# Three 64-byte gaps that move the split weights and the shared SBUF region of a one-core decoder kernel

## The chip, the cores and the metric

The kernel runs on one core of one Trainium2 chip. The metric is the device time in microseconds; the time before is the median of three runs, and one more execution was profiled.

## The reference

A trunk of two decoder layers on x of 256 rows by 1024 columns, float32. Each layer has a mixing part (RMSNorm, one input projection, a convolution group, an attention group, an output projection) and a channel part: a dense SwiGLU in layer 0, and in layer 1 a SwiGLU of which each row uses 2 of 8 experts.

```python
def swiglu(h, w1, w3, w2):
    return (jax.nn.silu(h @ w1) * (h @ w3)) @ w2

for layer in range(2):
    h = rms_norm(x, attn_norm_g[layer])
    z = h @ w_in[layer]
    ...
    x = x + jnp.concatenate([conv_out, attn_out], axis=-1) @ w_out[layer]
    h = rms_norm(x, ffn_norm_g[layer])
    if layer % 2 == 0:
        x = x + swiglu(h, dense_w1[i], dense_w3[i], dense_w2[i])    # 1024 -> 2816 -> 1024
    else:
        x = x + moe_swiglu(h, router_w[i], moe_w1[i], moe_w3[i], moe_w2[i])   # 8 experts, 1024 -> 3584 -> 1024
```

## The kernel before

All weights stream from HBM through `ring`, four slots of 16 KB a partition, which in the dense and the expert stage serve as seven pieces of 128 x 2048 float32. The SP queue issues the DMAs in one fixed order, each as soon as the piece's last tenant is used up.

The mixing parts use plain F32 matmuls on the ring, hT, mixT and the arena (L1120, L1163, L1309). The dense and the expert stage use F32R matmuls, in which each operand is split in a high and a low part and three products stand for one: high x high, high x low, low x high. For each piece ACT casts the high part into `w_hi` (L484), DVE subtracts it from the piece into `w_lo` (L734), and PE uses both. There are three buffers of each (`SPLIT` = 3): ACT waits for `w_used` of three pieces ago, DVE for ACT, PE for DVE. The order of this work on ACT and DVE is written out by hand, with the other work of the stage put between.

The operands that PE takes, written as stationary / moving:

- dense up, 352 of each line L1329 to L1331: a 128-column slice of w_hi or w_lo / hT_hi or hT_lo, 256 columns
- dense down, 88 of each line L1345 to L1347: a slice of dact_hi or dact_lo / w_hi or w_lo, 512 columns
- expert up, 896 of each line L1428 to L1430: a slice of xe_hi or xe_lo / w_hi or w_lo, 512 columns
- expert down, 448 of each line L1450 to L1452: a slice of actT_hi or actT_lo / w_hi or w_lo, 512 columns
- gather, L1384: a slice of h_hi or h_lo / sel, 256 columns
- scatter, L1403 and L1404: a slice of selT / ye_hi or ye_lo, 512 columns

Twelve matmuls use up one piece in expert up and down. Between the chunks stand transposes (L1438, L1101, which also fill waits so that PE stays busy).

SBUF tiles are laid out one behind the other in the order in which `sb` names them, each at the next multiple of 32 bytes in its partition: ring, w_hi, w_lo, x_sb, hn, hT, then the parameters, constants and small tables, the last of them vc. Behind vc comes one region that three sets of tiles share in turn: mixT and the arena for the mixing parts, hT_hi, hT_lo, dact_hi and so on for the dense stage, and h_hi, h_lo, xe_hi, xe_lo, actT_hi, actT_lo, ye_hi, ye_lo, sel, selT for the expert stage. All tiles there but the last have a size that is a multiple of 128 bytes, except the arena, which ends its set.

Of the kernel before, what the change touches and what calls it, by code (L numbers as in the profile page):

```python
# [5 lines left out]
P = 128  # L6
# [11 lines left out]
def hymba_trunk(nc, x, w_in, cmp_k_w1, cmp_v_w1, w_out, dense_w1, dense_w3, dense_w2,  # L18
# [74 lines left out]
    with ctx:  # L93
        def sb(name, shape, dt=F32):
            return ctx.enter_context(nc.sbuf_tensor(name, shape, dt))
# [2 lines left out]
            return ctx.enter_context(nc.semaphore(name))  # L98

        ring = sb("ring", [P, SLOTS * SLOT])  # L100
        w_hi = [sb(f"w_hi{n}", [P, PIECE], F32R) for n in range(SPLIT)]
        w_lo = [sb(f"w_lo{n}", [P, PIECE], F32R) for n in range(SPLIT)]
        x_sb = sb("x_sb", [P, NT, D])
        hn = sb("hn", [P, NT, D])
        hT = sb("hT", [P, KD, S])
# [36 lines left out]
        vc = sb("vc", [P, HD])  # L142


        attention_phase, dense_phase, expert_phase = ExitStack(), ExitStack(), ExitStack()


# [1404 lines left out]
```

How the kernel before makes its waits and increments, by code:

```python
        def wait_slot(eng, kind, l, c):  # L296
            n = slot_of[kind, l, c]
            eng.wait_ge(slot_arrived[n % SLOTS], 16 * turn_of[kind, l, c])
# [8 lines left out]
        def wait_raw(eng, t, j=None):  # L308
            eng.wait_ge(piece_arrived[t % RAW], nth(j, 16 * XS // RAW, 16 * (t // RAW + 1)))
# [24 lines left out]
        @block.sync  # L335
# [2 lines left out]
                sp.dma_start(x_sb[:, i, :], x[i * P:(i + 1) * P, :]).then_inc(x_loaded, 16)  # L338
            tenant = {}
            for key in stream:
                if key in slot_of:
                    n = slot_of[key]
                    parts, dst, arrived = (2 * (n % SLOTS), 2 * (n % SLOTS) + 1), slot(n), slot_arrived[n % SLOTS]
                else:
                    t = piece_of[key]
                    parts, dst, arrived = (t % RAW,), raw(t), piece_arrived[t % RAW]
                for before_it in dict.fromkeys(tenant[q] for q in parts if q in tenant):
                    sp.wait_ge(*last_read(before_it))
                tenant.update({q: key for q in parts})
                src, k, m = source(*key)
                dst = dst[:, 0:k * m].rearrange("p (k n) -> p k n", k=k)
# [9 lines left out]
            def stream_expert(j, e, first):  # L361
# [6 lines left out]
                    if first and m < RAW:  # L368
                        for before_it in dict.fromkeys([tenant[t % RAW]]):
                            sp.wait_ge(*last_read(before_it))
                    else:
                        sp.wait_ge(w_lo_ready, j * XS + (t - RAW + 1))
                    if kind == "e2":
```

## Time and profile before

| | us |
|---|---|
| median of 3 runs | 1643.5 (1641.4 to 1645.4) |
| the profiled execution | 1643.6 |
| its span | 1641.6 |
| PE busy | 1586.6 |
| DVE busy | 1194.1 |
| ACT busy | 908.1 |

The span runs from the first to the last instruction. PE is TensorE's matmuls, PEld its weight loads, DVE is VectorE, ACT ScalarE, POOL GpSimd. The two mixing parts lie at 0 to 200 and 400 to 600 us, the dense stage at 205 to 400, the expert stage at 615 to 1640. Matmuls overlap, and the end of each is modelled; what one costs is read from the distance between the starts of two that follow each other without a wait.

### The profile page before, as it was taken

To read this page: it belongs to the slowest core of one execution; us is meant where nothing else is said; L and a number is where in the kernel's file an instruction comes from. 1 tells how busy PE (TensorE), PEld (TensorE's weight loads), DVE (VectorE), ACT (ScalarE), POOL (GpSimd) and SP (SyncE) were. 2 spreads that over 40 slices of the span, in tenths; PEclk is the share of its full clock that TensorE was granted. 3 is DMA by queue.
4 is the path that set the end of the run, shared out by engine and by line. 5 is a ranking of instruction groups with operands and counts; after the bars stand their busy time and mean duration, and the time that the engine had idled before them with its cause. 6 is when DMAs were issued, how large, how long until landed. Compare 5 with 4: busy or idle time off the path is not lost.

```text
span 1641.6 us, 19740 instructions
## 1 busy us (share of the span) xinstructions
PE 1586.6 (97%) x7328; PEld 1227.3 (75%) x7328; DVE 1194.1 (73%) x1156; ACT 908.1 (55%) x834; POOL 24.0 (1%) x42
## 2 busy tenths in 40 slices
PE   7998999998999899999999999999999999999998
PEld 5663499997755367888887888887888887888886
DVE  4965155444775437889888889887889887888885
ACT  1034243342004316777777777777777777677674
POOL 1010000000010000000000000000000000000000
PEclk9978999999997799999999999999999999999999
DMA  7510195526070037999998999998999998999992
GB/s 242 197 37 0 44 340 180 182 100 196 15 254 27 0 129 253 361 366 346 357 371 304 359 366 351 357 367 301 364 363 347 363 360 318 356 360 358 356 347 99
DMA packets 203555, 426.56 MB, mean 260 GB/s; under 512 B 7378, under 2 KB 48594, under 8 KB 203476
## 3 DMA queue, kind: packets, MB, share of 16 engines
q1 hardware_dynamic: 202160, 424.90, 72.8%
q8 instruction: 64, 1.05, 0.3%
q10 hardware_dynamic: 1316, 0.49, 0.1%
q14 instruction: 15, 0.12, 0.0%
HBM read 424.31 MB, written 1.05 MB: 259 GB/s over the span
## 4 chain that ended last, share of the span: by engine, by line
PE 91%; DVE 4%; issue 2%; ACT 2%; DMA 1%; POOL 0%; ACTq 0%; POOLq 0%; DVEq 0%; SPq 0%
PE bank L1428 13%; PE bank L1430 13%; PE bank L1429 13%; PE bank L1120 8%; PE bank L1450 6%; PE bank L1452 6%; PE bank L1451 6%; PE bank L1309 3%; PE bank L1329 3%; PE bank L1331 3%; PE bank L1330 2%; PE bank L1264 2%; PE bank L1438 1%; PE bank L1345 1%; PE bank L1347 1%
## 5 line engine op out<-in xcount | busy, mean ns | idle before, releaser
L734 DVE TENSOR_TENSOR w_lo<-ring,w_hi 128x2048 fp32r<-128x2048 f32 x369 | 843.6, 2291 | 225.3 <-ACT w_hi L484 225.1
L484 ACT CAST w_hi<-ring 128x2048 fp32r<-128x2048 f32 x369 | 704.9, 1913 | 319.8 <-PE bank L1430 181.7
L1428 PE MATMUL bank<-w_hi,xe_hi 128*128 128x512 f32 x896 | 360.6, 402 | 6.8 <-DVE w_lo L734 6.8
L1429 PE MATMUL bank<-w_lo,xe_hi 128*128 128x512 f32 x896 | 355.0, 396 | 0.0
L1430 PE MATMUL bank<-w_hi,xe_lo 128*128 128x512 f32 x896 | 354.9, 396 | 0.0
L1428 PEld LDWEIGHTS bank<-w_hi,xe_hi 128*128 128x128 f32 x896 | 169.0, 189 | 46.6 <-DVE w_lo L734 8.4
L1430 PEld LDWEIGHTS bank<-w_hi,xe_lo 128*128 128x128 f32 x896 | 169.0, 189 | 41.2
L1429 PEld LDWEIGHTS bank<-w_lo,xe_hi 128*128 128x128 f32 x896 | 169.2, 189 | 38.1
L1450 PE MATMUL bank<-w_hi,actT_hi 128*128 128x512 f32 x448 | 177.8, 397 | 0.0
L1451 PE MATMUL bank<-w_lo,actT_hi 128*128 128x512 f32 x448 | 177.0, 395 | 0.0
L1452 PE MATMUL bank<-w_hi,actT_lo 128*128 128x512 f32 x448 | 177.0, 395 | 0.0
L1452 PEld LDWEIGHTS bank<-w_hi,actT_lo 128*128 128x128 f32 x448 | 84.1, 188 | 20.5
L1450 PEld LDWEIGHTS bank<-w_hi,actT_hi 128*128 128x128 f32 x448 | 84.2, 188 | 19.7
L1451 PEld LDWEIGHTS bank<-w_lo,actT_hi 128*128 128x128 f32 x448 | 84.2, 188 | 19.7
L1329 PE MATMUL bank<-hT_hi,w_hi 128*128 128x256 f32 x352 | 98.4, 280 | 0.0
L1330 PE MATMUL bank<-hT_lo,w_hi 128*128 128x256 f32 x352 | 98.1, 279 | 0.0
L1331 PE MATMUL bank<-hT_hi,w_lo 128*128 128x256 f32 x352 | 98.1, 279 | 0.0
L757 DVE SCALAR_TENSOR_TENSOR arena<-arena,par 128x256 f32<-128x256 f32 x240 | 96.2, 480 | 0.1
L729 DVE TENSOR_TENSOR x_sb<-x_sb,bank 128x512 f32<-128x512 f32 x48 | 30.3, 683 | 66.8 <-PE bank L1309 60.0
L1120 PE MATMUL bank<-ring,hT 128*128 128x512 f32 (+1 forms) x192 | 72.3, 531 | 0.0
L1329 PEld LDWEIGHTS bank<-hT_hi,w_hi 128*128 128x128 f32 x352 | 66.1, 188 | 0.4
L1330 PEld LDWEIGHTS bank<-hT_lo,w_hi 128*128 128x128 f32 x352 | 65.9, 187 | 0.4
(228 smaller groups left out, 1457.7 us busy)
## 6 DMA issues: line engine op xcount, KB each, us to landing
ring<-in_moe_w SPq DMA_DIRECT2D x336, 1024.0 KB, 5.7
ring<-in_dense_w SPq DMA_DIRECT2D x33, 1024.0 KB, 5.4
ring<-in_w_in SPq DMA_DIRECT2D x8, 1024.0 KB, 9.6
ring<-in_w_in SPq DMA_DIRECT2D x4, 2048.0 KB, 14.3
ring<-in_w_out SPq DMA_DIRECT2D x4, 2048.0 KB, 14.3
ring<-in_cmp_k_w SPq DMA_DIRECT2D x2, 2048.0 KB, 17.2
ring<-in_cmp_v_w SPq DMA_DIRECT2D x2, 2048.0 KB, 8.8
ring<-in_w_in SPq DMA_DIRECT2D x2, 1120.0 KB, 15.6
```

The lines of the kernel that those rows point to most:

```text
L484: nc.scalar.copy(w_hi[t % SPLIT][:], raw(t)).then_inc(w_hi_ready, 1)
L734: V.tensor_tensor(w_lo[t % SPLIT][:], raw(t), w_hi[t % SPLIT][:].bitcast(F32), ALU.subtract).then_inc(w_lo_ready, 1)
L1120: last = T.matmul(dst, lhs(k), rhs(k), start=(n == 0), stop=(n == len(chunks) - 1))
L1329: T.matmul(dst, hi[:, k, c], hT_hi[:, k, :], start=(k == 0), stop=False)
L1330: T.matmul(dst, hi[:, k, c], hT_lo[:, k, :], start=False, stop=False)
L1331: last = T.matmul(dst, lo[:, k, c], hT_hi[:, k, :], start=False, stop=(k == KD - 1))
L1428: T.matmul(dst, xe_hi[:, kk, own], hi[:, k, :], start=(kk == 0), stop=False)
L1429: T.matmul(dst, xe_hi[:, kk, own], lo[:, k, :], start=False, stop=False)
L1430: last = T.matmul(dst, xe_lo[:, kk, own], hi[:, k, :], start=False, stop=(kk == KD - 1))
L1450: T.matmul(dst, actT_hi[:, c % 2, f], hi[:, k, r], start=first, stop=False)
L1451: T.matmul(dst, actT_hi[:, c % 2, f], lo[:, k, r], start=False, stop=False)
L1452: last = T.matmul(dst, actT_lo[:, c % 2, f], hi[:, k, r], start=False, stop=end)
```

## The change

Three tiles of 64 bytes a partition that nothing reads or writes are allocated: one between the ring and the split weights, one between the split weights and x_sb, and one between vc and the region that the stages share. With them the split weights begin 64 bytes above a multiple of 128, where they began at one, and the shared region begins at a multiple of 128. x_sb and all up to vc move by 128 bytes.

```diff
         ring = sb("ring", [P, SLOTS * SLOT])
+        sb("split_gap", [P, 16])
         w_hi = [sb(f"w_hi{n}", [P, PIECE], F32R) for n in range(SPLIT)]
         w_lo = [sb(f"w_lo{n}", [P, PIECE], F32R) for n in range(SPLIT)]
+        sb("x_gap", [P, 16])
         x_sb = sb("x_sb", [P, NT, D])
...
         vc = sb("vc", [P, HD])


+        sb("gap", [P, 16])
         attention_phase, dense_phase, expert_phase = ExitStack(), ExitStack(), ExitStack()
```

## Rows read from the trace of the kernel before

**Rows 1.** The page: busy us of each engine, share of the span, instructions
```profile
PE 1586.6 (97%) x7328; PEld 1227.3 (75%) x7328; DVE 1194.1 (73%) x1156; ACT 908.1 (55%) x834; POOL 24.0 (1%) x42
```
**Rows 2.** Stretches; columns: stretch, us, busy by engine, PEclk, DMA share, GB/s
```profile
185.00:330.00 145.00, 143.62 (x1008) 129.03 (x1007) 69.94 (x52) 57.76 (x47) 1.11 (x2) 1.00 0.66 216
...
640.00:1640.00 1000.00, 990.02 (x4446) 801.21 (x4444) 851.16 (x510) 714.73 (x510) 0.00 (x0) 1.00 0.95 342
```
**Rows 3.** Groups by line and shape: count, busy us, mean ns, idle before
```profile
L734 DVE TENSOR_TENSOR w_lo<-ring,w_hi 128x2048 fp32r<-128x2048 f32 x369 | 843.6, 2291 | 225.3 <-ACT w_hi L484 225.1
...
L1428 PE MATMUL bank<-w_hi,xe_hi 128*128 128x512 f32 x896 | 360.6, 402 | 6.8 <-DVE w_lo L734 6.8
...
L1450 PE MATMUL bank<-w_hi,actT_hi 128*128 128x512 f32 x448 | 177.8, 397 | 0.0
...
L1329 PE MATMUL bank<-hT_hi,w_hi 128*128 128x256 f32 x352 | 98.4, 280 | 0.0
...
L1345 PE MATMUL bank<-w_hi,dact_hi 128*128 128x512 f32 x88 | 34.8, 395 | 0.0
```
**Rows 4.** Timeline of PE and PEld, expert up: start us, us, instruction; five matmuls left out
```profile
700.01 0.39 PE L1429 MATMUL bank<-w_lo,xe_hi 128*128 128x512 f32 x1
700.01 0.19 PEld L1430 LDWEIGHTS bank<-w_hi,xe_lo 128*128 128x128 f32 x1
...
701.41 0.39 PE L1429 MATMUL bank<-w_lo,xe_hi 128*128 128x512 f32 x1
```
**Rows 5.** Timeline of PE, dense down; two matmuls left out
```profile
269.73 0.39 PE L1345 MATMUL bank<-w_hi,dact_hi 128*128 128x512 f32 x1
...
270.43 0.39 PE L1345 MATMUL bank<-w_hi,dact_hi 128*128 128x512 f32 x1
```
**Rows 6.** Timeline of PE, dense up, first stretch; five matmuls left out
```profile
212.01 0.28 PE L1329 MATMUL bank<-hT_hi,w_hi 128*128 128x256 f32 x1
...
212.69 0.28 PE L1329 MATMUL bank<-hT_hi,w_hi 128*128 128x256 f32 x1
```
**Rows 7.** Timeline of PE, dense up, a later stretch; eight matmuls left out
```profile
259.88 0.28 PE L1329 MATMUL bank<-hT_hi,w_hi 128*128 128x256 f32 x1
...
260.94 0.28 PE L1329 MATMUL bank<-hT_hi,w_hi 128*128 128x256 f32 x1
```
**Rows 8.** Timeline of PE, scatter and what follows; four matmuls left out
```profile
761.30 0.39 PE L1404 MATMUL bank<-ye_lo,selT 128*128 128x512 f32 x1
...
762.43 0.40 PE L1428 MATMUL bank<-w_hi,xe_hi 128*128 128x512 f32 x1
```
**Rows 9.** Timeline of PE, gather, merged by the view
```profile
613.80 1.00 PE L1384 MATMUL bank<-sel,h_hi 128*128 128x256 f32 x7
614.64 1.12 PE L1384 MATMUL bank<-sel,h_lo 128*128 128x256 f32 x8
```
**Rows 10.** Timeline of PE, plain F32 matmuls of the input projection
```profile
51.92 7.07 PE L1120 MATMUL bank<-hT,ring 128*128 128x256 f32 x32
```
**Rows 11.** Single lines of DVE and ACT: ns min/median/max, first and last start
```profile
L757 DVE SCALAR_TENSOR_TENSOR arena<-arena,par x240: 468/480/486, 32.1 to 496.5; 128x256 f32<-128x256 f32 x120
...
L935 DVE TENSOR_TENSOR hT_lo<-hT,hT_hi x4: 686/690/691, 204.3 to 206.1; 128x512 fp32r<-128x512 f32 x4
...
L942 DVE TENSOR_TENSOR dact_lo<-dact,dact_hi x11: 684/685/695, 223.9 to 385.5; 128x512 fp32r<-128x512 f32 x11
...
L591 ACT CAST hT_hi<-hT x4: 617/619/622, 202.6 to 204.4; 128x512 fp32r<-128x512 f32 x4
...
L600 ACT CAST dact_hi<-dact x11: 612/614/622, 221.8 to 384.9; 128x512 fp32r<-128x512 f32 x11
```
**Rows 12.** Timeline of DVE and PE, expert down: a piece ready and used
```profile
901.66 2.29 DVE L734 TENSOR_TENSOR w_lo<-ring,w_hi 128x2048 fp32r<-128x2048 f32 x1 [0.35 <-ACT w_hi L484]
...
905.11 0.39 PE L1450 MATMUL bank<-w_hi,actT_hi 128*128 128x512 f32 x1
```
**Rows 13.** One stretch of 2 us, the DMA's GB/s last
```profile
900.00:902.00 2.00, 2.00 (x10) 1.64 (x9) 1.65 (x3) 1.63 (x1) 0.00 (x0) 1.00 1.02 413
```

## The prediction

> **What bounds the kernel now.** I first read the page's busy times: PE is busy for 1586.6 us, 97% of the span [rows 1]. The table by stretches then separates the stages. In the expert stage PE is busy for 990 of 1000 us at clock 1.00 (the 2.4 GHz level), DVE for 851, ACT for 715. In the dense stage, 185 to 330 us, PE is busy for 143.6 of 145 [rows 2]. So each nanosecond of the spacing of PE's matmuls there is a nanosecond of the span, unless a feeder becomes late. The groups say how many there are [rows 3]: L1428 to L1430 have 896 each and L1450 to L1452 448 each, 4032 matmuls of 512 columns in the expert stage; L1345 to L1347 have 88 each, 264 of 512 columns in the dense stage; L1329 to L1331 have 352 each, 1056 of 256 columns. The idle time before L1428, the largest PE group, is 6.8 us in all.
>
> The mean of one matmul in those groups (402 ns) is not its cost, since matmuls overlap. The cost is the distance between starts, from the timeline.
>
> **What the change moves.** It has no instruction, wait or DMA more or less. By the change's own words the six split-weight tiles go from 0 to 64 bytes above a multiple of 128, and the shared region goes to 0. The tiles between them (x_sb to vc) take 41,792 bytes, each rounded up to 32; that is 326.5 times 128, so before it the shared region lies at 64. The ring, x_sb, hn and hT lie at 0 before and after (x_gap puts the last three back). Every slice that a matmul takes starts a multiple of 512 bytes into its tile, so a tile's place is that of all its slices.
>
> The split matmuls (F32R) have these places before, written as stationary/moving operand:
> - expert up and down, and dense down: 64/0 (xe, actT or dact / weights), 512 columns. In the timeline 6 matmuls take 1.40 us from start to start, 0.2333 each [rows 4], and 0.70 for 3, 0.2333 [rows 5].
> - dense up: 0/64 (weights / hT_hi, hT_lo), 256 columns. In the first stretch, entered from the 50 transposes, 0.68 for 6, 0.1133 [rows 6]; in the later ones, entered from dense down, 1.06 for 9, 0.1178 [rows 7]. One instruction stream with two spacings at one clock and with the same tiles: two things inside PE meet in step, and which step depends on how the stretch was entered. What PE reads together are the moving operand and the next stationary one: the LDWEIGHTS of L1430 starts with the matmul of L1429 [rows 4].
> - scatter: 64/64 (selT / ye), 512 columns: settles at 1.13 for 5, 0.226 [rows 8].
> - gather: 64/64 (h / sel), 256 columns: 0.84 for 7, 0.120 [rows 9].
>
> After it, expert up, expert down and dense down are 0/64, dense up is 64/0, scatter and gather are 0/0.
>
> **The cost of a matmul, split.** Scatter and gather have the same places and differ by 256 columns: 0.226 - 0.120 = 0.106 us for 256 columns, and that is 256 clocks of 2.4 GHz (0.1067), one for each column; the 0.014 left is then the same at both widths. Expert up and dense up differ by 0.2333 - 0.1178 = 0.1155, more than the clocks: either their pairs differ in the extra, or it grows with columns. Taking 0.106 or 0.212 off the others leaves, per matmul: 64/0 0.0213; 0/64 0.0073 or 0.0118; 64/64 0.014. So the placement with the moving operand at 0 costs most, and the one with it at 64 and the stationary one at 0 costs least. I take the first of the two readings, an extra for each weight load beside a running stream that depends on the pair, because at 64/64 it doesn't grow.
>
> **The sum**, against the profiled execution (span 1641.6 us, run 1643.6, median of the runs 1643.5, so the run stands for the median):
> - 4032 + 264 = 4296 matmuls of 512 columns go from 64/0 to 0/64. This pair with 512 columns is not in the trace. Bounds: 0.212 + 0.0073 = 0.2193 below and 0.240 above (twice gather's 0.120). I take 0.212 + 0.0118 = 0.2238, from the nearest row that is entered like most of them, out of other split matmuls. Gain 0.0095 x 4296 = 40.8 us (60.1 at 0.2193).
> - 1056 matmuls of dense up go from 0/64 to 64/0, also not in the trace with 256 columns. Now they cost 192 x 0.1133 + 864 x 0.1178 = 123.5 us. With the extra of 64/0, 0.106 + 0.0213 = 0.1273, they cost 134.4: a loss of 10.9. Half of 0.2333, 0.1167, is the other bound: 123.2, a gain of 0.3. I take the loss, since it follows from the same reading as the gain.
> - 160 gather and 72 scatter matmuls go to 0/0. Between 0.0073 and 0.0213 of extra against 0.014 now, that is 1.6 us either way; I take 0.
> - The plain F32 matmuls of the attention stages: 256 columns take 7.07 us for 32, about 0.22 each, twice the F32R price [rows 10]. Columns pass at half the rate there, and L1120 has hT and the ring both at 0, unmoved. Those on mixT and the arena move by 64 bytes against the ring; I take 0.
> - DVE and ACT: the 240 taps of L757 start at every fourth byte and take 468 to 486 ns. A subtraction with inputs at 0 and 64 has a median of 690 ns, with both at 64 685; a cast from 0 to 64 619, from 64 to 64 614 [rows 11]. So L734 and L484, which now go from the ring at 0 to weights at 64, change by some 5 ns (of 2291 for L734 [rows 3]). That hides under PE: one w_lo piece is written by 903.95 and PE comes to it at 905.11, 1.16 us later [rows 12]. Two pieces of 12 matmuls pass between the release of a buffer and its need; with 0.2238 that shortens the time by 24 x 0.0095 = 0.23 us and leaves 0.9.
> - DMA writes the ring where it did. A piece of 1.05 MB per 12 matmuls is 374 GB/s now and 390 at 0.2238; one 2 us stretch reached 413 [rows 13]. The mean over the stage would go from 342 to some 356. This doesn't bind; at 0.2193 (398 in such stretches) it comes near.
>
> Net: 40.8 - 10.9 = 29.9, so 1643.6 - 29.9 = 1613.7 us. With 0.2193 it is 1643.6 - 60.1 + 10.9 = 1594.4. If the place of the stationary operand doesn't matter (extra 0.014, spacing 0.226), the gain is 0.0073 x 4296 - 10.9 = 20.5: 1623.1. The forecast's own range is 1594 to 1625.
>
> **The rivals.**
> Same. Only whether the two operands lie on the same or on different halves counts, and 64/0 and 0/64 are different halves alike. Then the extra at different halves grows with columns (0.0213 at 512, 0.0073 to 0.0118 at 256, about half), and the change swaps one for the other: 1643 to 1644 us. For it: dense up is close to half of expert up (0.1178 x 2 = 0.2356, 0.1133 x 2 = 0.2267, around 0.2333). Against it: a cost that grows with columns for one pair and not for the other is an odd law.
> The Trainium skill would also have it so. "SBUF — State Buffer", Who interferes with whom, says that PE never waits on anyone at its two independent read ports, and "TensorE: Matmul & The Clock Gate", Back-to-back issue gap, gives N/2.4 + 2.5 ns, 215.8 ns for 512 columns warm, whatever the addresses. The trace doesn't agree: 233.3 ns at granted clock 1.00 [rows 2, 4], and 226 in another placement [rows 8]. By the pages' rule the change does nothing.
>
> Slower. The extra goes with the pair 0/64 in proportion to the columns, at the rate of dense up's later stretches: 2 x 0.1178 = 0.2356 for 512. The place is the 4296 long matmuls: 0.0023 x 4296 = 9.9 us, less 0.3 in dense up: 1653.2. At gather's rate, 0.240, it is 0.0067 x 4296 = 28.8: 1672. It decides as soon as the long matmuls settle above 0.2333. For it: dense up's later stretches are nine of ten.
>
> Faster by another law. Proportional too, but in the step of dense up's first stretch: 2 x 0.1133 = 0.2266, a gain of 0.0067 x 4296 = 28.8, 1615, without a loss in dense up.
>
> **How the numbers follow.** Forecast 0.43, faster by the other law 0.10, same 0.29, slower 0.18. A measurement of this kernel can tell about 0.2% (3.3 us) from no change: faster by more than that 0.53, within it 0.29, slower 0.18. The likeliest case gives 1614. The range goes from 1592, a little under the forecast's low end, to 1652, nearly the nearer point of the slower case: beyond it lies most of the slower case, 0.14, and below it 0.03.
>
> **What would show it.** Starts of L1428 to L1430 at 0.219 to 0.226 apart (same: 0.2333; slower: 0.2356 and up); L1345 to L1347 alike; L1329 to L1331 at 0.127 (by the other laws 0.117); DVE's and ACT's durations as before; PE's idle time before L1428 still under some 10 us. If that idle time grows with DVE or DMA named, the feeders took the gain. What would make the forecast wrong is the step from 256 columns to 512: that the extra of 0/64 is paid once per weight load is read off the 64/64 rows and carried over.

## The result, and the profile after

| | before | after |
|---|---|---|
| median, us | 1642.45 (4 runs, 1641.33 to 1645.38) | 1621.79 (4 runs, 1613.29 to 1625.08) |
| the profiled execution, us | 1643.6 | 1624.96 |
| its span, us | 1641.6 | 1622.9 |

The ratio is 0.9872, with a 95% interval of 0.9833 to 0.9911: the change makes the kernel 20.7 us faster at the medians. A second measurement (e6) gives 1621.13 against 1640.83, ratio 0.9883 (0.9854 to 0.9913).

The three new lines push the code down, so L1428 of before is L1431 here, L1450 is L1453, L1329 is L1332, L1345 is L1348, L734 is L737. The page's busy times, which answer to [rows 1]:

```profile
PE 1567.8 (97%) x7328; PEld 1225.5 (76%) x7328; DVE 1193.3 (74%) x1156; ACT 906.1 (56%) x834; POOL 24.0 (1%) x42
```

PE lost 18.8 us of busy time, and the span 18.7. DVE, ACT and the number of instructions are as before. The stretch of the expert stage that answers to the second line of [rows 2], and the groups that answer to [rows 3]:

```profile
640.00:1640.00 1000.00, 971.30 (x4435) 799.24 (x4433) 848.10 (x506) 712.47 (x510) 0.00 (x0) 1.00 0.94 341
```
```profile
L737 DVE TENSOR_TENSOR w_lo<-ring,w_hi 128x2048 fp32r<-128x2048 f32 x369 | 843.0, 2290 | 207.5 <-ACT w_hi L487 207.3
L487 ACT CAST w_hi<-ring 128x2048 fp32r<-128x2048 f32 x369 | 702.5, 1906 | 303.6 <-PE bank L1433 172.6 <-PE bank L1455 75.4 <-PE bank L1334 27.9
L1431 PE MATMUL bank<-w_hi,xe_hi 128*128 128x512 f32 x896 | 357.3, 399 | 7.0 <-DVE w_lo L737 7.0
```

The granted clock is 1.00 as before. The stretch now reaches past the end of the kernel, so PE's 971.3 us are no idle time. DVE's subtraction takes 2290 ns (2291 before), and PE's idle time before the largest group is 7.0 us (6.8): no feeder became late. What changed is the spacing of starts. The timeline of PE, expert down and then dense up (start us, duration us; 14 and 11 matmuls left out):

```profile
699.70 0.40 PE L1453 MATMUL bank<-w_hi,actT_hi 128*128 128x512 f32 x1
...
703.13 0.39 PE L1453 MATMUL bank<-w_hi,actT_hi 128*128 128x512 f32 x1
```
```profile
262.75 0.28 PE L1332 MATMUL bank<-hT_hi,w_hi 128*128 128x256 f32 x1
...
264.11 0.28 PE L1332 MATMUL bank<-hT_hi,w_hi 128*128 128x256 f32 x1
```

15 long matmuls take 3.43 us, 0.2287 each, where [rows 4, 5] have 0.2333. 12 of dense up take 1.36, 0.1133 each, where [rows 7] have 0.1178. Over all matmuls, starts behind a wait or a transpose left out, the means from start to start are 229.2 ns in expert up, 229.0 in expert down, 228.9 in dense down (233.3 in all three before), and 113.6 in dense up (117.1 before). So the long ones give (233.3 - 229.1) x 4296 = 18 us and dense up (117.1 - 113.6) x 1056 = 3.7 us, 21.7 in all. From the first to the last expert matmul the time falls from 1007.6 to 991.5 us (16.1), from the first to the last of dense up from 173.9 to 169.4 (4.5, with the dense down in it). The rest of the difference of the two spans, 1.9 us the other way, lies in the mixing parts, whose time differs by more than that from one execution of a kernel to the next: from the last matmul of the dense stage to the first gather it is 218.8 us in this execution of the changed kernel and 213.8 in e6's.

Gather has kept its 0.120: in the timeline around 611 us twelve start in 1.44 us.

### The profile page after: what moved, and what is told of

It reads as the page before. It is cut to its first block, busy times and chain, and to the rows that moved or that the text cites. A ratio compares the mean times of both kernels' runs of the same rounds, so it can differ in the third digit from the quotient of the medians.

```text
span 1622.9 us, 19740 instructions
## 1 busy us (share of the span) xinstructions
PE 1567.8 (97%) x7328; PEld 1225.5 (76%) x7328; DVE 1193.3 (74%) x1156; ACT 906.1 (56%) x834; POOL 24.0 (1%) x42
## 4 chain that ended last, share of the span: by engine, by line
PE 90%; DVE 4%; ACT 2%; issue 2%; DMA 1%; POOL 0%; ACTq 0%; POOLq 0%; DVEq 0%; SPq 0%
PE bank L1431 13%; PE bank L1433 13%; PE bank L1432 13%; PE bank L1123 8%; PE bank L1455 6%; PE bank L1453 6%; PE bank L1454 6%; PE bank L1312 3%; PE bank L1332 2%; PE bank L1334 2%; PE bank L1333 2%; PE bank L1267 2%; PE bank L1441 2%; PE bank L1235 1%; PE bank L1350 1%
## 5 line engine op out<-in xcount | busy, mean ns | idle before, releaser
L737 DVE TENSOR_TENSOR w_lo<-ring,w_hi 128x2048 fp32r<-128x2048 f32 x369 | 843.0, 2290 | 207.5 <-ACT w_hi L487 207.3
L487 ACT CAST w_hi<-ring 128x2048 fp32r<-128x2048 f32 x369 | 702.5, 1906 | 303.6 <-PE bank L1433 172.6
L1431 PE MATMUL bank<-w_hi,xe_hi 128*128 128x512 f32 x896 | 357.3, 399 | 7.0 <-DVE w_lo L737 7.0
L1432 PE MATMUL bank<-w_lo,xe_hi 128*128 128x512 f32 x896 | 351.2, 392 | 0.0
L1431 PEld LDWEIGHTS bank<-w_hi,xe_hi 128*128 128x128 f32 x896 | 169.1, 189 | 42.8 <-DVE w_lo L737 8.5
L1453 PE MATMUL bank<-w_hi,actT_hi 128*128 128x512 f32 x448 | 176.1, 393 | 0.0
L1332 PE MATMUL bank<-hT_hi,w_hi 128*128 128x256 f32 x352 | 97.4, 277 | 0.0
L1453 PEld LDWEIGHTS bank<-w_hi,actT_hi 128*128 128x128 f32 x448 | 84.2, 188 | 17.3
L1332 PEld LDWEIGHTS bank<-hT_hi,w_hi 128*128 128x128 f32 x352 | 66.1, 188 | 0.4
```

Source lines behind the costliest of these rows:

```text
L487: nc.scalar.copy(w_hi[t % SPLIT][:], raw(t)).then_inc(w_hi_ready, 1)
L737: V.tensor_tensor(w_lo[t % SPLIT][:], raw(t), w_hi[t % SPLIT][:].bitcast(F32), ALU.subtract).then_inc(w_lo_ready, 1)
L1332: T.matmul(dst, hi[:, k, c], hT_hi[:, k, :], start=(k == 0), stop=False)
L1431: T.matmul(dst, xe_hi[:, kk, own], hi[:, k, :], start=(kk == 0), stop=False)
L1432: T.matmul(dst, xe_hi[:, kk, own], lo[:, k, :], start=False, stop=False)
L1453: T.matmul(dst, actT_hi[:, c % 2, f], hi[:, k, r], start=first, stop=False)
```

## Experiments

Below, a place is a byte address modulo 256. The distance of a matmul is the place of its stationary operand less that of its moving one, modulo 256. This is not how the prediction looked at it, but it is what the runs led to:

| kernel | weights | region | long matmuls, distance | dense up, distance |
|---|---|---|---|---|
| before | 128 | 192 | 64 | 192 |
| after | 192 | 128 | 192 | 64 |
| e1: weights alone | 192 | 64 | 128 | 128 |
| e2: region alone | 128 | 0 | 128 | 128 |
| e3: all by 128 | 0 | 64 | 64 | 192 |

The expectations of e1, e2, e5, e7 and e8 take the places of e1 or e2 for distance 0. That was my error: modulo 128 both tiles lie at one place, modulo 256 they lie 128 apart.

**Parts of the change.** e1 leaves out the gap ahead of the region, e2 keeps only that one, e3 has one gap of 128 bytes ahead of the weights and keeps every place modulo 128.

```diff
 # e1, against the kernel after
-        sb("gap", [P, 16])
 # e2, against the kernel after
-        sb("split_gap", [P, 16])
-        sb("x_gap", [P, 16])
 # e3, against the kernel before
+        sb("split_gap", [P, 32])
```

> The third gap is left out: the split weights go to 64, the shared region stays at 64, so all split matmuls are 64/64 (stationary/moving). Pair theory (each pair of places has its own spacing): the long matmuls come near the scatter row of before, 0.226 to 0.2296, span 1612 to 1627; dense up near gather, 0.120, 3 us more than before. Moving-operand theory (only the place of the moving operand counts, 64 is the good one for 512 columns): the long ones 0.229 as with both changes, span 1623 or less. Relative theory (only same or different halves, or the distance between the two): another spacing than the 0.229 of the full change, since here the distance is 0.

> Only the third gap: the weights stay at 0, the shared region goes to 0, so all split matmuls are 0/0. Pair theory: a spacing of its own, between 0.219 and 0.240. Moving-operand theory: the long matmuls stay at 0.2333, span 1640 to 1644. Relative theory: the same spacing as with the weights alone moved (distance 0 in both), for the long and for the dense-up matmuls.

> One gap of 128 bytes ahead of the split weights: all but the ring moves by 128, so the halves stay 64/0 and 0/64 as before, and only the place modulo 256 turns. If the place modulo 128 is what counts: 0.2333 and 0.1133 to 0.1178, time as before within 0.2%. If the place modulo 256 or the distance to the ring counts: another spacing, or other durations on DVE and ACT.

e1: 1638.16 us, ratio 1.0008 (0.9975 to 1.0042). e2: 1636.55, ratio 0.9987 (0.9969 to 1.0005). e3: 1640.71, ratio 0.9998 (0.9977 to 1.0018); before 1641.4. Neither half of the change makes a measurable difference alone. The long matmuls (those of 512 columns) have means of 232.2 to 233.1 ns in e1, 232.2 to 232.5 in e2, 233.3 in e3; dense up is at 118.7, 118.7 and 117.1. Weights and region each moved on their own bring no gain, the two together do: what counts is a relation between the two operands, not the place of either. e3 has the spacings of before to 0.1 ns, so moving weights and region together by 128 is free.

**The price of pairs.** e4 puts nineteen trains of 96 equal matmuls behind the last scatter of the kernel before, where ACT, DVE and the DMA queues are idle. A train is one uninterrupted row of matmuls, entered from four transposes (`keep_busy`); its settled spacing is the mean from start to start once it repeats itself. The first train:

```diff
+            keep_busy(4, 4)
+            for _ in range(96):
+                T.matmul(bank[0][0:128, 0:512], probe_s[:, 0:128], probe_w[:, 0:512], start=True, stop=True)
...
```

> The kernel before, with 19 trains of 96 equal F32R matmuls appended on PE behind the last scatter, each entered from four transposes: eleven pairs of places of stationary and moving operand at 512 columns, four at 256, and two with a stationary operand of 32 columns instead of 128; nothing else runs then. About 390 us longer. Pair theory with an extra per weight load: 64/0 at 512 columns 0.2333, 0/64 0.224 to 0.229, 64/64 0.226; at 256 columns the same extras (0.127, 0.113, 0.120); with 32-column loads the extra falls to a quarter. Extra that grows with columns: 0.1167 at 256 columns, and 0.2333 with 32-column loads too. Relative theory: trains of the same distance but other places have the same spacing. If DVE, ACT or DMA make the extra, all trains come at 0.2133 to 0.216.

Four trains, by line (columns: duration ns min/median/max, first and last start us):

```profile
L1501 PE MATMUL bank<-w_hi,xe_hi x96: 393/396/478, 1630.2 to 1652.4; 128*128 128x512 f32 x96
...
L1507 PE MATMUL bank<-w_hi,xe_hi x96: 388/392/481, 1675.8 to 1697.7; 128*128 128x512 f32 x96
...
L1510 PE MATMUL bank<-w_hi,xe_hi x96: 387/389/476, 1698.2 to 1719.9; 128*128 128x512 f32 x96
...
L1552 PEld LDWEIGHTS bank<-w_hi,xe_hi x96: 107/108/112, 1971.3 to 1993.2; 128*32 128x32 f32 x96
L1552 PE MATMUL bank<-w_hi,xe_hi x96: 391/396/478, 1971.3 to 1993.4; 128*32 128x512 f32 x96
```

Stationary and moving operand lie at 448 and 128 (modulo 512) in L1501, at 64 and 128 in L1507, at 128 and 128 in L1510. The settled spacings are 233.3, 228.9 and 226.7 ns. L1501 and L1507 are one pair of halves, 64 and 0 modulo 128, and differ by 4.4 ns: the reading by halves is wrong. All trains of 512 columns at 32-byte places agree with the distance: 64 gives 233.3 (448/128, 448/384 has 64 too, 0/192), 192 gives 228.9 (64/128, 128/192, 128/448), 0 gives 226.7 (128/128, 448/448, 448/192), 128 gives 233.4 (0/128). L1552 loads 32 columns of weights in place of 128. The load takes 108 ns, not 188, yet the train settles at 231.7: the extra does not shrink with the load, and is no fixed price for each one. The other train with 32-column loads has distance 192 and settles at 231.7 too, so with the short load these two distances, 4.4 ns apart with the full one, make no difference.

**The distances.** e5 has the form of the kernel: three products to a slice, both operands walking in steps of 512 words, at twelve distances and three widths. The first train:

```diff
+            for n in range(32):
+                k, m = 512 * (n % 3) + 48, 512 * (n % 3)
+                for sv, wv in ((ph, wh), (ph, wl), (pl, wh)):
+                    T.matmul(bank[0][:, 0:512], sv[:, k:k + 128], wv[:, m:m + 512], start=True, stop=True)
...
```

> The kernel before with 23 trains of 96 matmuls behind the last scatter, each in the expert's own pattern (high x high, high x low, low x high, on changing slices of xe and w): twelve distances stationary minus moving modulo 256 at 512 columns, eight at 256, three at 384. Distance theory (formed after the single-pair trains: distance 0 226.7, 64 233.3, 128 233.4, 192 228.9 ns at 512 columns; 64 113.3, 192 117.8, 0 120.0 at 256): distances 64, 128 and 192 repeat these numbers in the pattern, and the distances between give values of their own. If the 232.5 ns of the region-only kernel at distance 0 come from the pattern of three products, distance 0 gives about 232.5 here too; if they come from DVE, ACT or DMA working beside PE, it gives 226.7. Extra per column: 384 columns at distance 64 175.0, at 192 171.7. Extra per matmul: 180.0 at 64 and 175.5 at 192.

Timeline of PE, distances 0, 64 and 192 at 512 columns (11 matmuls left out of each pair):

```profile
1647.40 0.39 PE L1503 MATMUL bank<-w_lo,xe_hi 128*128 128x512 f32 x1
...
1650.12 0.39 PE L1503 MATMUL bank<-w_lo,xe_hi 128*128 128x512 f32 x1
...
1714.52 0.40 PE L1518 MATMUL bank<-w_hi,xe_lo 128*128 128x512 f32 x1
...
1717.32 0.40 PE L1518 MATMUL bank<-w_hi,xe_lo 128*128 128x512 f32 x1
...
1827.36 0.39 PE L1543 MATMUL bank<-w_lo,xe_hi 128*128 128x512 f32 x1
...
1830.11 0.39 PE L1543 MATMUL bank<-w_lo,xe_hi 128*128 128x512 f32 x1
```

Twelve matmuls take 2.72, 2.80 and 2.75 us: 226.7, 233.3 and 229. The whole table of settled spacings, in ns:

| distance | 0 | 16 | 32 | 64 | 96 | 128 | 160 | 176 | 192 | 208 | 224 | 240 |
|---|---|---|---|---|---|---|---|---|---|---|---|---|
| 512 columns | 226.7 | 226.7 | 233.3 | 233.3 | 234.3 | 233.4 | 233.3 | 230.1 | 228.8 | 233.3 | 233.3 | 226.7 |
| 384 columns | 173.3 | | | 174.7 | | | | | 173.3 | | | |
| 256 columns | 120.0 | | 118.4 | 113.3 | 118.7 | 118.7 | 120.1 | | 117.8 | | 116.7 | |

Taking the clocks of the columns off (N/2.4 at granted clock 1.00), distance 0 leaves 13.3 ns at all three widths. Distance 64 leaves 6.6, 14.7 and 20.0 at 256, 384 and 512 columns, distance 192 leaves 11.1, 13.3 and 15.5. So the extra is neither one price nor in proportion: it depends on distance and width together. The best distance for 256 columns (64) is among the worst for 512. One train stands behind each cell. The values of 0, 64 and 192 at 512 columns came again in each train of e4, e7 and e11 that has these distances at places that are multiples of 32 bytes; for 16, 128 and 240 the runs below show a second value each.

**Is it the company?** In the kernel DVE, ACT and the queues write SBUF beside PE. e7 runs trains alone and beside DVE subtractions, ACT casts and 1 MB DMAs into the ring, one by one and together. ACT's part beside the third train:

```diff
...
+            sc.wait_ge(go, 3)
+            for q in range(10):
+                nc.scalar.copy(w_hi[2][:], raw(1)).then_inc(abusy, 1)
+                sc.wait_ge(abusy, 0 + q + 1)
...
```

> The kernel before with 14 trains of 96 matmuls of 512 columns in the expert's pattern behind its end, at one distance each, alone or beside nine DVE subtractions (D), ten ACT casts (A), eight DMAs of 1 MB into the ring (S) of the kernel's own kind. Theory that the 232.5 ns of the region-only kernel at distance 0 are the doing of another engine beside PE: distance 0 gives 226.7 alone and about 232.5 beside the one that disturbs it, and 64 and 192 stay at 233.3 and 228.9 with all three. Rival: the other engines do nothing (the rule that PE waits on nobody), and distance 0 gives 226.7 in all five trains; then the kernel's 232.5 is a step that PE fell into by how it was entered.

Two stretches of trains at distance 192, first beside all three, then beside the DMAs alone or none (busy us of PE, PEld, DVE, ACT, POOL; granted clock, DMA share, GB/s), and the timeline of PE in the first:

```profile
1888.00:1906.00 18.00, 18.00 (x81) 14.75 (x80) 17.76 (x8) 17.71 (x10) 0.00 (x0) 1.00 0.78 272
1866.00:1884.00 18.00, 18.00 (x81) 14.75 (x80) 0.00 (x0) 0.00 (x0) 0.00 (x0) 1.00 0.66 233
```
```profile
1895.42 0.39 PE L1699 MATMUL bank<-w_lo,xe_hi 128*128 128x512 f32 x1
...
1898.16 0.39 PE L1699 MATMUL bank<-w_lo,xe_hi 128*128 128x512 f32 x1
```

The second stretch was meant to be alone, but its trace has DMA traffic of 233 GB/s, left over from the train before; e4 and e5 have the same spacings with no traffic at all. PE starts 81 matmuls in 18 us in both, with DVE and ACT busy throughout in one and idle in the other. With nothing else at work (e5) and beside all three: 226.7 and 226.7 at distance 0, 233.3 and 233.3 at 64, 228.8 and 228.9 at 192; distance 0 keeps 226.7 beside each of the three alone as well. At these distances the spacing is PE's own affair. For two others that isn't shown. Distance 128 settles at 232.4 beside all three where e5 has 233.4, and distance 240 at 228.3 where e5 has 226.7, on the same addresses. Neither ran alone in e7. Both hold their value from the first microsecond to the last, and other runs below have two values at one distance with nothing beside PE, so a second rhythm is as likely a reason as the company. Here the Trainium skill holds ("SBUF — State Buffer", Who interferes with whom: PE waits on nobody), as far as other engines go at those three distances. That the two read ports which the same section gives PE are independent is what the trains don't bear out: with PE alone at work, another relation of its two operands' addresses costs 7 ns more.

**Gains that the distance promises.** e9 is the changed kernel with two more gaps, so that the long matmuls have distance 0 and dense up keeps its 64. e10 puts weights and region at one place, 192, so that all have 0. e8 has distance 16, which was as good as 0 in e5, with the weights at 176 and all behind them 256 bytes further on.

```diff
 # e9, against the kernel after
         hT_hi, hT_lo = ...
+        sb_d("dense_gap", [P, 16])
         dact_hi, dact_lo = ...
         h_hi, h_lo = ...
+        sb_e("expert_gap", [P, 16])
         xe_hi = ...
 # e10, against the kernel after
-        sb("x_gap", [P, 16])
+        sb("x_gap", [P, 48])
-        sb("gap", [P, 16])
 # e8, against the kernel before: tiles that may start at 16 bytes
+        sb("split_gap", [P, 12])
-        w_hi = [sb(f"w_hi{n}", [P, PIECE], F32R) for n in range(SPLIT)]
...
+        w_hi = [sb16(f"w_hi{n}") for n in range(SPLIT)]
...
```

> The split weights 48 bytes above their place of before and everything behind them 256 bytes, so that the long matmuls have distance 16 modulo 256, and dense up 240. If a train's spacing alone carries over: 226.7 for the long matmuls, 28 us less than before, dense up some 3 us more, span about 1615. If distances near 0 are disturbed in the kernel as 0 was: 232 to 233, span 1635 to 1642.

> The changed kernel with two more gaps of 64 bytes, one ahead of dact_hi and one ahead of xe_hi: the long matmuls get distance 0 modulo 256 (all places multiples of 32 bytes), dense up keeps 64. Distance theory: long 226.7, dense up 113.3; 4296 x 2.2 ns less than the changed kernel is 9.5 us, so about 1612, ratio to before 0.981 to 0.984. If the long ones don't settle at 226.7 in the kernel (as at distance 16, where they came at 233.3 and 236.7), 1620 to 1650.

> Weights 64 bytes on, everything behind them 256 bytes on: distance 0 modulo 256 in all split matmuls, both operands at the same place. Distance theory: long 226.7, dense up 120.0: 28.4 less, 2.8 to 3.1 more, about 1617. Half theory (same half 64/64): what the weights-only kernel gave, 1634 to 1640.

e9: 1618.98 us, ratio 0.9866 (0.9849 to 0.9883). e10: 1617.25, ratio 0.9861 (0.9828 to 0.9894). e8: 1647.52, ratio 1.0036 (1.0021 to 1.0051). First and last start of expert up in before, after, e9 and e10 (L1428 under the line number of each):

```profile
L1428 PE MATMUL bank<-w_hi,xe_hi x896: 393/394/797, 623.4 to 1615.1; 128*128 128x512 f32 x180
```
```profile
L1431 PE MATMUL bank<-w_hi,xe_hi x896: 388/394/795, 621.0 to 1596.7; 128*128 128x512 f32 x180
```
```profile
L1433 PE MATMUL bank<-w_hi,xe_hi x896: 388/390/792, 624.3 to 1593.2; 128*128 128x512 f32 x180
```
```profile
L1430 PE MATMUL bank<-w_hi,xe_hi x896: 387/389/795, 622.2 to 1589.7; 128*128 128x512 f32 x180
```

991.7, 975.7, 968.9 and 967.5 us: the expert stage is 7 to 8 us shorter than in the changed kernel, as 226.7 against 228.9 ns promises, and the means there are 227.0 to 227.6. But e10 pays 120.0 ns in dense up, 6.4 x 1056 = 7 us back, and e9 did not keep its 113.3. Dense up in e9, first stretch and a later one (8 and 11 matmuls left out):

```profile
214.15 0.28 PE L1336 MATMUL bank<-hT_hi,w_lo 128*128 128x256 f32 x1
...
215.17 0.28 PE L1336 MATMUL bank<-hT_hi,w_lo 128*128 128x256 f32 x1
```
```profile
262.83 0.28 PE L1336 MATMUL bank<-hT_hi,w_lo 128*128 128x256 f32 x1
...
264.24 0.28 PE L1336 MATMUL bank<-hT_hi,w_lo 128*128 128x256 f32 x1
```

0.1133 in the first, 0.1175 in the later one, with w_hi and hT_hi at the very places of the changed kernel. All nine later stretches settle at 117.8, which costs 9 x 96 x 4.4 = 3.8 us. e10 came out as its spacings promise. e9 came out 7 us above the 1612 that was expected of it: these 3.8, and some 3 us because its long matmuls have means of 226.9 to 227.6 and not 226.7. Neither kernel is shown to beat the changed one: the three ratios' intervals overlap.

e8 is slower than before where its distance promised a gain, and shows that a train doesn't always speak for the kernel. Between one group of transposes and the next lie 164 stretches of expert matmuls, 12 to 48 long; 99 of them settle at 236.7 ns and 65 at 233.3:

```profile
699.76 0.40 PE L1457 MATMUL bank<-w_hi,actT_lo 128*128 128x512 f32 x1
...
703.31 0.40 PE L1457 MATMUL bank<-w_hi,actT_lo 128*128 128x512 f32 x1
```

15 matmuls in 3.55 us. e11 asked whether 16-byte places are a case of their own.

```diff
...
+                k, m = 512 * (n % 3) + 0, 512 * (n % 3) + 12
...
```

> Ten trains of 96 matmuls of 512 columns in the expert's pattern behind the kernel before, at places (stationary, moving) modulo 256. Theory from the distance-16 kernel: distance alone counts only while the moving operand starts at a multiple of 32 bytes. (192,192) 226.7, (208,192) 226.7, (192,176) 233.3 to 236.7, (176,176) and (144,128) tell whether the moving or the stationary operand has to be so placed; (192,132) above 236, (196,128) near 233; (64,128) 228.9, (64,144) above it. If only the distance counts: (192,176), (208,192) and (144,128) all 226.7.

Partly. Stationary/moving at 192/176, the places of e8, gives 226.7 again, so the train still doesn't show what the kernel does. But distance 16 at 208/192 and at 144/128 gives 233.4, and distance 0 at 176/176 gives 230.0 against 226.7 at 192/192. At 192/132, the moving operand 4 bytes past a multiple of 16, it is 240.0; at 196/128, the stationary one 4 bytes past, 231.4. But the train at 144/128 is e5's train of distance 16 over again: the same instructions on the same addresses, entered from four transposes, with nothing beside PE. There it settled at 226.7. First e5, then e11, 11 matmuls left out of each pair:

```profile
1668.25 0.39 PE L1508 MATMUL bank<-w_lo,xe_hi 128*128 128x512 f32 x1
...
1670.97 0.39 PE L1508 MATMUL bank<-w_lo,xe_hi 128*128 128x512 f32 x1
...
1712.00 0.40 PE L1518 MATMUL bank<-w_lo,xe_hi 128*128 128x512 f32 x1
...
1714.80 0.40 PE L1518 MATMUL bank<-w_lo,xe_hi 128*128 128x512 f32 x1
```

2.72 against 2.80 us for twelve. So neither the distance nor the places settle the spacing here, and e8's miss need not be a matter of 16-byte places: a train shows one rhythm of those that its addresses allow. Ahead of the four transposes stood a train at 226.7 in e5 and one at 230.0 in e11.

**Two rhythms at one distance.** e12 asks what e9's dense up has that the changed kernel's has not. Its trains have dense up's form at distances 64 and 192 and start behind transposes alone or behind eighteen long matmuls of four distances.

```diff
...
+            keep_busy(4, 4)
+            long(0, 16)    # eighteen of 512 columns, distance 0
+            for n in range(32):
+                k = 256 * (n % 7)
+                for wv, hv in ((wh, ph), (wh, pl), (wl, ph)):
+                    T.matmul(bank[0][:, 0:256], wv[:, k + 32:k + 32 + 128], hv[:, k:k + 256], start=True, stop=True)
...
```

> The kernel before with thirteen trains of 96 matmuls of 256 columns behind its last scatter, in the dense up's form (stationary a slice of the split weights, moving the split activations, three products to a slice). The question is why the dense up of the two-distances kernel settled at 117.8 ns and that of the changed kernel at 113.4, with w_hi and hT_hi at the same places (distance 64) in both, and why in the kernel before the first stretch has 113.3 and the nine others 117.8 at one distance (192). The trains at distance 64 and at distance 192 start behind four transposes alone, or behind eighteen matmuls of 512 columns at distance 0, 64, 192 or 128. If the distance alone sets the spacing: 113.3 in all trains at 64, 117.8 in all at 192, whatever stands ahead. If one distance carries two rhythms and the matmuls ahead choose between them: at 64, 117.8 behind distance 0 and 113.3 behind distance 192; at 192, 117.8 behind distance 64; some of the others differ among themselves. If something else in the kernel does it (the buffers of the down matmuls, the waits): one value a distance, as under the first. In two trains (64 behind 0, 192 behind 64) a matmul of 384 columns stands in the middle: under two rhythms the spacing may change there, under distance alone it is the same on both sides. At distance 0 behind distance 64: 120.0 under both.

Distance 64, behind long matmuls of distance 0 (L1514) and of distance 64 (L1520), 11 left out of each pair:

```profile
1657.20 0.28 PE L1514 MATMUL bank<-xe_hi,w_lo 128*128 128x256 f32 x1
...
1658.62 0.28 PE L1514 MATMUL bank<-xe_hi,w_lo 128*128 128x256 f32 x1
...
1673.09 0.28 PE L1520 MATMUL bank<-xe_hi,w_hi 128*128 128x256 f32 x1
...
1674.45 0.28 PE L1520 MATMUL bank<-xe_hi,w_hi 128*128 128x256 f32 x1
```

1.42 against 1.36 us for twelve, the same instructions on the same addresses. At distance 64 the train settles at 113.3 behind transposes, behind 64 and behind 128, at 117.8 behind 0 and behind 192, and keeps it to its end; a matmul of 384 columns put in the middle doesn't move it. At distance 192 all trains have 117.8. So one distance can carry two stable rhythms, and what stood ahead chooses between them. This is e9's case: its dense down has distance 0. It is no full law. In the changed kernel dense up at 64 comes behind dense down at 192 and has 113.4 where the train has 117.8, and in the kernel before the first stretch at 192 has 113.3 [rows 6], a rhythm that no train at 192 took. Nor is it only the short ones: in the changed kernel 3 of the 164 expert stretches settle at 233.3 and the others at 228.6 to 229.2, and the train at 144/128 has both 226.7 and 233.3.

**The changed kernel again**, in a second measurement:

> The changed kernel again, on one chip with many runs of the kernel before: ratio 0.983 to 0.991 if the first measurement holds. If the gain hangs on the chip or on how PE falls into step in one execution, it differs from that.

1621.13 us, ratio as given at the top; 229.2, 229.0, 228.8 and 113.6 ns, as in the first measurement.

## Why the prediction was right, and where it was not

1614 was forecast with a range of 1592 to 1652; 1621.8 came out, faster, inside the forecast's own range. The steps:

- **PE sets the end, and each nanosecond of spacing counts**: right. 18.8 us of PE's busy time went, 18.7 of the span, and the idle time before the largest group is 7.0, 6.8 before.
- **DVE, ACT, DMA, gather at nothing**: right. 2290 against 2291 ns for the subtraction, 1906 against 1913 for the cast, 347 against 348 GB/s between 640 and 1620 us, gather 0.120.
- **The cost of a matmul, split.** This is the step that failed. It took the extra as a price for each weight load that depends on the pair of halves modulo 128. e4 has two trains with one pair of halves and 4.4 ns between them (L1501 and L1507), and a weight load of 108 ns in place of 188 that leaves the extra nearly whole. What the runs show in its place, for places at multiples of 32 bytes, is the distance of the two starts modulo 256, with a different extra at each width, and at some distances a choice of two rhythms. The fixed 0.014 read off scatter and gather was real (13.3 ns at three widths), but it belongs to distance 0 alone and could not be carried to another pair.
- **The long matmuls at 0.2238, gain 40.8**: direction right, size over twice too large. They settle at 228.9, for 18 us. The term was 0.0118 of extra, from dense up at distance 192; at 512 columns that distance costs 0.0155. The warning at the end of the prediction, that the step from 256 to 512 columns was the weak one, names it.
- **Dense up at 0.1273, loss 10.9**: wrong in sign. It gains 3.7. With 256 columns distance 64 leaves 6.6 ns in this kernel, not 21.3. That gain is not the distance's alone: at the same places nine of e9's ten stretches leave 11.1, as before the change. The two misses offset each other in part: 22.8 too much and 14.6 too little, so the total came out 8 us off while its largest term was 23 off. That the time lies so well inside the range is in part luck.
- **If the place of the stationary operand doesn't matter, 1623.1**: nearest in time, and wrong too. In e1 the weights, which the long matmuls take as moving operand, lie as in the changed kernel, and the long ones stay at 232.2 to 233.1.
- **Two spacings of one stream, by how it was entered**: right. The prediction read it off [rows 6, 7], and e12 shows it.
- **The rival "same"**: e1 and e2 are the test that it needed, since they move the operands without exchanging them, and they show that other moves do leave the time. But the changed kernel is faster, clear of the noise. By the 215.8 ns that the Trainium skill's formula gives for 512 columns ("TensorE: Matmul & The Clock Gate", Back-to-back issue gap, there for the isolated gap of one matmul) nothing should have moved; the lowest of any train of 512 columns here is 226.7, at granted clock 1.00.
- **The rival "slower"**: 0.2356 for 0/64 did not come; 0.2367 did come in e8, at a 16-byte place.
- **"Faster by another law"**: 0.2266 is the spacing of distance 0 (e10), which the change didn't choose. Its 0.1133 in dense up came true. The law itself, in proportion to columns, is wrong: distance 64 is best at 256 and among the worst at 512.

What stays open: why the distance acts so. That PE's running matmul and the next weight load read SBUF together, and fall into a rhythm by which they meet more or less often, would go with two rhythms on one set of addresses, but no run shows the reads themselves. Open too are which start leads to which rhythm, how far back what ran ahead still counts, and whether DVE, ACT or the DMAs have a part in it at distances 128 and 240.

## What to carry to other kernels

When PE is the bound and its matmuls stand back to back, measure the distance between starts for each kind of matmul, and compare it between kinds and stretches of one width; 1 to 3% can lie in nothing but where the two operands start. A gap of 64 bytes in the right place costs no time and moves all later tiles: for F32R matmuls try both operands at one place modulo 256 with 512 columns and the stationary one 64 above the moving one with 256, and judge a placement in the kernel, since neighbours can choose the rhythm. Don't carry a price from one width or pair to another; a train of each form, put behind the kernel's work, gives it in one run.

## What the runs showed of the hardware

- An F32R matmul of 512 columns, full stationary operand, starts 226.7 to 234.3 ns after the one before it, by the distance of the operands' starts modulo 256, with both at multiples of 32 bytes; of 256 columns 113.3 to 120.1 ns (e4, e5, at granted clock 1.00). Moving both by 128 changes nothing (e3).
- Beside DVE, ACT and DMAs of 272 GB/s the spacings at distances 0, 64 and 192 are the same to 0.1 ns as without them (e5, e7). At 128 and 240 they differ by 1.0 and 1.6 ns, cause open.
- The same instructions on the same addresses run at 113.3 or 117.8 ns over a whole train of 256 columns, by what ran ahead of them (e12), and at 226.7 or 233.3 ns over a train of 512 columns at 144/128 (e5, e11).
- A weight load of 32 columns takes 108 ns where one of 128 takes 188, and the matmuls start 1.6 ns closer at distance 64 and 2.8 ns further apart at distance 192, at 231.7 in both (e4).
- With the moving operand 4 bytes past a multiple of 16 (192/132) the spacing is 240.0 ns, the longest of all trains of 512 columns here (e11); with both 4 bytes past, at distance 64 (452/132), it is 236.1, against 233.3 for distance 64 otherwise (e4).
